# A two-block transformer kernel: the first two output chunks run together behind y, and the end of the memory attention runs inside the first latent head's gate product

## The chip, the cores and the metric

The kernel runs on one core of a Trainium2 chip. The metric is the device time of one execution in microseconds. Three executions of the kernel before took 2343.36, 2345.44 and 2347.05 us, a median of 2345.44.

## The reference

The input is 512 tokens of width 2048. Block one is a pre-norm layer of sliding-window attention with sinks (32 query heads of 64, 4 key heads), a SiLU gate and an output matrix. Block two has two layers, each of latent attention (8 heads of 128 + 64), a short convolution and an attention over 256 memory tokens (4 heads), which are concatenated, gated and multiplied by an output matrix. Cut to what matters here:

```python
# block one
y = (o.astype(z.dtype) * jax.nn.silu(z)) @ w_out
x = x + rmsnorm(y, g_post[i])
# block two, layer l
q = (rmsnorm_2(q_lat, q_norm_g[l]) @ w_uq[l]).reshape(b, s, MLA_HEADS, QK_HEAD_DIM)
kv = (rmsnorm_2(kv_lat, kv_norm_g[l]) @ w_ukv[l]).reshape(b, s, MLA_HEADS, QK_NOPE_DIM + V_HEAD_DIM)
a_out = mla_attention(q, k, v)
m_out = memory_attention(q_mem.reshape(b, s, MEM_HEADS, MEM_HEAD_DIM), mem_n, w_mk[l], w_mv[l])
y = jnp.concatenate([a_out, c_out, m_out], axis=-1) * jax.nn.silu(gate)
o = y @ w_o[l]
x = x + rmsnorm_2(o, post_norm_g[l])
```

## The kernel before, in words

Activations lie transposed: 16 tiles of 128 features by 512 tokens (`KT` = 16). Every product is written as three matmuls on halves of the operands: each operand is split into `hi` (rounded to fp32r) and `lo` (the remainder), and TensorE (PE) adds hi·hi, hi·lo and lo·hi (`passes`, L415). Weights come in chunks of 128 output features by 2048 input features, 1 MB each. SyncE loads a chunk into one of two slots (`raw`), ScalarE (ACT) writes `hi` (`split`, L758), VectorE (DVE) writes `lo` (`split`, L1082), and PE runs 48 matmuls over it (`features`). A chunk that uses a slot must wait until PE has finished the chunk before last. PE's result lies in one of two accumulators in PSUM (`acc`) until ACT or DVE has read it (`evacuated`).

The orders of all engines are written out by hand and are tied by counting semaphores. An engine takes its instructions strictly in its own order, so a wait holds all that stands behind it.

Three places matter for the change.

The start of an output product (three times: behind block one, behind layer 0 and behind layer 1 of block two). The gated outputs y stand in `g`, 16 tiles. ACT writes `h_hi` from them (`y_hi_tile`, L768), DVE writes `h_lo` (`y_lo_tile`, L1258), and PE multiplies. `h_hi` and `h_lo` hold the normed input h until then, and the last gate's product reads h up to its end, so ACT waits for the end of it. PE's first output chunk waits for each y tile in turn (`ready`); the second one runs its 32 matmuls on hi weights first and its 16 on lo weights last (`features_low_last`, L429 to L433). Before them stand the values of the last pair or head (`values_first`, L549; `values_head`, L721), which give the last y tile.

The first latent head of each layer. Its projection (`project`) makes the head's queries and keys from the latents, 18 matmuls, and, for two heads at once, the rotary queries and the values in banks of `sc`, 36 matmuls. These banks hold the scores of the last memory head until then. So PE first transposes the last memory head's probabilities (`turn_mem`, L650) as soon as DVE has scaled them (L1471), and waits until ACT has copied the result to `ptm` (L1000). Behind the projection come the memory values (`values_mem`, L657), the first gate product of the head, the scores (`scores_head`, L701 and L702) and the second gate product, with the transposes of the head's probabilities before its tile 12 (`turn_head`, L710).

DVE's order in that head: the lo split of the first gate's weights, the rotation of the queries (L1481 to L1486), the lo parts of keys, queries and rotary queries (L1500 to L1504), the lo split of the second gate's weights, the copy of the memory values (L1460), the first gate's evacuation (L1513), the lo split of the next head's weights, the gate (L1519), the maximum of the scores (L1521) and the scaling of the probabilities (L1527). ACT's exponentials (L1043) lie between these two.

Of the kernel before, what the change touches and what calls it, by code (L numbers as in the profile page):

```python
# [22 lines left out]
def build(nc, xT, memT, mem, pos, gains, sinks, consts, window, w1, w2, out):  # L23
# [89 lines left out]
    FIRST_SQUARES = SQUARES[:2]  # L113

# [12 lines left out]
    with ctx:  # L127
# [104 lines left out]
        y_hi_done, y_done = sem("y_hi_done"), sem("y_done")  # L232
# [172 lines left out]
        def _(pe):  # L405
# [168 lines left out]
            features(z_b, h_hi, h_lo, meanwhile=[(13, lambda: turn_first(B))])  # L574
            values_first(B)

            def out_product(l):

                features(chunk2(l, WO), h_hi, h_lo, ready=lambda j: pe.wait_ge(y_done, l * KT + (j + 1)))
                features_low_last(chunk2(l, WO + 1), h_hi, h_lo)  # L580
                with pe.Fori(1, KT // 2) as i:
                    for p in range(2):
                        features(chunk2(l, WO + p, i, 2), h_hi, h_lo)

            with pe.Fori(0, LAYERS) as l:
# [85 lines left out]
                def project(c, j, free_banks):  # L672

                    begin(c)
                    w_hi, w_lo = hi[c.slot], lo[c.slot]

                    def product(to, at, x, first, last, w_moves=False):
                        w = slice(at, at + (2 * P if w_moves else P))
                        return passes(to, w_hi[:, w], w_lo[:, w], m_hi[:, x], m_lo[:, x], first, last, w_moves)

                    for k in range(QRT):
                        product(acc[c.slot][:, :], k * QW[j], tile(KVRT + k), k == 0, k == QRT - 1)
                    for k in range(KVRT):
                        ins = product(ov[1][:, :], UK[j] + k * P, tile(k), k == 0, k == KVRT - 1)
                    if j == 0:
                        free_banks()
                        for k in range(QRT):
                            product(bank(0), k * QW[j] + P, tile(KVRT + k), k == 0, k == QRT - 1)
                        for b in range(TB):
                            for k in range(KVRT):  # L690
                                ins = product(bank(1 + b // 2, 2 * P, b % 2 * 2 * P), UV + k * 2 * P,
                                              slice(k * S + b * P, k * S + (b + 1) * P), k == 0, k == KVRT - 1, True)
                    ins.then_inc(chunk_done, 1)
# [30 lines left out]
                def end_of_memory():  # L724
                    turn_mem(MH - 1)
                    pe.wait_ge(ptm_done, l * MH + MH)

                def head(i, j, first=False):

                    no = l * MLA + (i * 2 + (j + 1))  # L730
                    project(chunk2(l, HEAD + 3 * j, i, 6), j, end_of_memory if first else lambda: turned_read(no - 1))
                    if first:
                        values_mem(MH - 1)
                    else:
                        values_head(no - 1, 1 - j)
                    features(chunk2(l, HEAD + 3 * j + 1, i, 6), h_hi, h_lo)
                    scores_head(no, i, j)
                    features(chunk2(l, HEAD + 3 * j + 2, i, 6), h_hi, h_lo, meanwhile=[(12, lambda: turn_head(no))])
# [4 lines left out]
                with pe.Fori(1, MLA // 2) as i:  # L743
                    head(i, 0)
                    head(i, 1)
                values_head(l * MLA + MLA, 1)
# [6 lines left out]
        def _(act):  # L753
# [109 lines left out]
            turned_first(B, B + 1)  # L863
            tanh_first(B, z_b)

            def y_hi_tiles(nxt, last_ready):

                with act.Fori(0, KT // 2) as t:
                    y_hi_tile(t)
# [5 lines left out]

            act.wait_ge(y1, PAIRS)
            act.wait_ge(chunk_done, N1)
            act.wait_ge(x_stored, 16)
# [34 lines left out]
            with act.Fori(0, LAYERS) as l:  # L913
# [103 lines left out]
                def head(i, j, first=False, last=False):  # L1017
# [27 lines left out]
                    ins.then_inc(exp2, 1)  # L1045
                    act.wait_ge(turned2, no)
# [32 lines left out]
        def _(dve):  # L1079
# [158 lines left out]
            def gate_first(i, zc):  # L1238
                dve.wait_ge(chunk_done, zc.n + 1)
                dve.tensor_tensor(zt[:, :], acc[zc.slot][:, :], r_x[:, :], ALU.mult).then_inc(evacuated[zc.slot], 1)  # L1240
                dve.wait_ge(tanh1, i + 1)
# [47 lines left out]
            split(chunk2(0, WO + 1))  # L1289

# [35 lines left out]
            with dve.Fori(0, LAYERS) as l:  # L1326
# [161 lines left out]
                def head(i, j, first=False, last=False):  # L1488
# [39 lines left out]
                    ins.then_inc(probs2, 1)  # L1528
                    dve.wait_ge(turned2, no)
# [4 lines left out]
                    dve.tensor_tensor(dg[:, :], acc[gb.slot][:, :], r_h, ALU.mult).then_inc(evacuated[gb.slot], 1)  # L1534
                    dve.wait_ge(tanh2, no * 2)
# [134 lines left out]
```

## Time and profile before

| | |
|---|---|
| median of three executions | 2345.44 us |
| the profiled execution's own time | 2344.45 us |
| its span | 2342.6 us |
| PE busy | 2277.9 us (97%) |
| DVE busy | 1186.3 us (51%) |
| ACT busy | 798.8 us (34%) |
| GpSimd busy | 184.2 us (8%) |
| moved by DMA | 238.98 MB, mean 102 GB/s |
| mean granted clock of PE | 0.993 |

The span is that of the core; the execution's own time is 1.9 us longer. PE's busy time counts matmuls, whose durations overlap in a stream. Starts and ends in the timelines are microseconds from the span's start; what stands in brackets behind a row is the idle time of that engine before it and the instruction that ended it. The output products of block one, layer 0 and layer 1 start near 503, 1316 and 2133 us; the first latent heads start near 1002 and 1821 us.

### The profile page before, as it was taken

Reading aid. Unit: us, or ns where it says so; the run is one execution under the profiler, and the core shown is the slowest. Engines: PE = TensorE matmul, PEld = TensorE weight load, DVE = VectorE, ACT = ScalarE, POOL = GpSimd, SP = SyncE. Lnnn points to the kernel's source line nnn. Section 1 sums busy time; section 2 is a strip of 40 time slices with the busy share of each in tenths; the row PEclk is TensorE's granted clock in tenths of the full one; section 3 lists DMA queues with packets and bytes.
Section 4 is the critical chain, followed back from the end, with each engine's and each line's share of the span. In section 5 each row is a group of like instructions: output and inputs, shape, how many; then the busy total and the mean of one; then the engine's idle time right before and its main releaser. Section 6 shows DMA issues by size and latency. Waiting matters only on the chain.

```text
span 2342.6 us, 28762 instructions
## 1 busy us (share of the span) xinstructions
PE 2277.9 (97%) x10726; PEld 1863.3 (80%) x10726; DVE 1186.3 (51%) x1531; ACT 798.8 (34%) x1216; POOL 184.2 (8%) x172
## 2 busy tenths in 40 slices
PE   7999999999999999999999999999999999999995
PEld 6888888878888888878877788878888787877884
DVE  7666666772238543445455532475433544554124
ACT  5443434352335411332333322344113323333220
POOL 4111111101110100000000011101000000000113
PEclk9999999999999999999999999999999999999997
DMA  7321222223237232212221222462322221213221
GB/s 282 113 72 72 72 83 78 76 98 114 90 142 263 81 108 90 70 61 78 75 87 57 113 91 106 150 246 72 108 90 72 75 79 59 87 66 138 107 90 72
DMA packets 36648, 238.98 MB, mean 102 GB/s; under 512 B 4192, under 2 KB 4448, under 8 KB 12896
## 3 DMA queue, kind: packets, MB, share of 16 engines
q1 hardware_dynamic: 29808, 204.47, 24.2%
q10 hardware_dynamic: 6336, 25.17, 2.8%
q0 software_dynamic: 432, 8.39, 0.9%
q8 instruction: 44, 0.72, 0.1%
q14 instruction: 28, 0.23, 0.0%
HBM read 221.24 MB, written 16.78 MB: 102 GB/s over the span
## 4 chain that ended last, share of the span: by engine, by line
PE 85%; DVE 7%; ACT 4%; issue 2%; DMA 1%; ACTq 0%; SPq 0%; POOL 0%; DVEq 0%; POOLq 0%
PE acc L415 68%; PE sc L415 4%; PE ov L721 2%; PE ov L415 2%; PE sc L710 1%; ACT hi L758 1%; ACT prob L1043 1%; PE ov L549 1%; PE sc L537 1%; DMA raw<-w_dram 1%; DVE lo L1082 1%; PE acc L429 1%; PE acc L430 1%; PE acc L433 1%; DVE st L1521 1%
## 5 line engine op out<-in xcount | busy, mean ns | idle before, releaser
L415 PE MATMUL acc<-h_hi,hi 128*128 128x512 f32 x2480 | 985.3, 397 | 27.3 <-DVE h_lo L1144 15.0
L415 PE MATMUL acc<-h_lo,hi 128*128 128x512 f32 x2480 | 967.8, 390 | 0.0
L415 PE MATMUL acc<-h_hi,lo 128*128 128x512 f32 x2480 | 967.5, 390 | 0.0
L1082 DVE TENSOR_TENSOR lo<-raw,hi 128x2048 fp32r<-128x2048 f32 (+2 forms) x196 | 432.7, 2208 | 492.1 <-ACT hi L758 489.8
L415 PEld LDWEIGHTS acc<-h_hi,hi 128*128 128x128 f32 x2480 | 467.1, 188 | 135.5 <-issue 28.8
L415 PEld LDWEIGHTS acc<-h_lo,hi 128*128 128x128 f32 x2480 | 467.2, 188 | 98.7 <-issue 5.3
L415 PEld LDWEIGHTS acc<-h_hi,lo 128*128 128x128 f32 x2480 | 466.8, 188 | 98.2
L758 ACT ACTIVATE hi<-raw 128x2048 fp32r<-128x2048 f32 (+2 forms) x196 | 361.5, 1844 | 275.2 <-PE acc L415 225.5
L765 ACT ACTIVATE sq<-acc 128x512 f32<-128x512 f32 x48 | 28.7, 599 | 358.5 <-PE acc L415 334.7
L827 ACT ACTIVATE prob<-prob,st 128x256 f32<-128x256 f32 x128 | 63.3, 496 | 136.6 <-DVE st L1204 136.6
L321 POOL TENSOR_TENSOR sqacc<-sqacc,sq 128x512 f32<-128x512 f32 x42 | 54.6, 1300 | 402.4 <-ACT sq L765 402.4
L1043 ACT ACTIVATE prob<-sc,st 128x512 f32<-128x512 f32 x64 | 43.2, 689 | 80.6 <-DVE st L1522 80.6
L1036 ACT ACTIVATE sq<-sq 128x512 f32<-128x512 f32 x16 | 10.1, 632 | 142.4 <-DVE sq L1513 142.4
L721 PE MATMUL ov<-prob,v 128*128 128x512 f32 x128 | 57.5, 592 | 0.0
L1513 DVE TENSOR_TENSOR sq<-acc,g 128x512 f32<-128x512 f32 x16 | 11.1, 692 | 84.0 <-PE acc L415 84.0
L325 POOL TENSOR_TENSOR sqacc<-sq 128x512 f32<-128x512 f32 x3 | 3.9, 1290 | 544.2 <-ACT sq L765 544.2
L415 PE MATMUL sc<-hi,m_hi 128*128 128x256 f32 (+1 forms) x128 | 43.2, 337 | 0.8 <-DVE lo L1082 0.8
L377 POOL COPY vcur<-vall 128x256 f32 x32 | 20.0, 650 | 297.4 <-PE ov L549 297.0
L390 POOL DMA_DIRECT2D area<-memT_dram x2 | 1.2, 612 | 535.5 <-ACT h_hi L768 535.5
L415 PE MATMUL sc<-lo,m_hi 128*128 128x256 f32 (+1 forms) x128 | 43.0, 336 | 0.0
L415 PE MATMUL sc<-hi,m_lo 128*128 128x256 f32 (+1 forms) x128 | 43.0, 336 | 0.0
L821 ACT ACTIVATE q<-dg 64x512 fp32r<-64x512 f32 x32 | 20.2, 630 | 66.4 <-DVE dg L1230 66.2
(217 smaller groups left out, 2489.3 us busy)
## 6 DMA issues: line engine op xcount, KB each, us to landing
raw<-w_dram SPq DMA_DIRECT2D x172, 1024.0 KB, 4.7
xr<-residual ACTq DMA_DIRECT2D x16, 512.0 KB, 5.7
residual<-g ACTq DMA_DIRECT2D x16, 512.0 KB, 4.2
raw<-w_dram SPq DMA_DIRECT2D x8, 896.0 KB, 4.4
raw<-w_dram SPq DMA_DIRECT2D x8, 768.0 KB, 5.4
g<-xT_dram SPq DMA_DIRECT2D x4, 1024.0 KB, 11.3
residual<-g POOLq DMA_DIRECT2D x1, 4096.0 KB, 13.8
area<-memT_dram POOLq DMA_DIRECT2D x2, 2048.0 KB, 9.2
```

What stands on the lines that cost most here:

```text
L321: pool.tensor_tensor(to[:, :], to[:, :], sq[:, tile(slot)], ALU.add).then_inc(added, 1)
L415: ins = pe.matmul(to, a, b, start=first and n == 0, stop=last and n == 2)
L429: pe.matmul(to, w_hi[:, tile(k, P)], x_hi[:, tile(k)], start=k == 0, stop=False)
L430: pe.matmul(to, w_hi[:, tile(k, P)], x_lo[:, tile(k)], start=False, stop=False)
L433: ins = pe.matmul(to, w_lo[:, tile(k, P)], x_hi[:, tile(k)], start=False, stop=k == KT - 1)
L537: ins = pe.transpose(bank(kb, P, par * 256 + nxt * P), prob1[:, src:src + P], ident)
L721: ins = pe.matmul(ov[0][:, :], v[:, (2 * k + j) * P:(2 * k + j + 1) * P], prob2[:, tile(k)], start=k == 0, stop=k == TB - 1)
L758: act.activation(hi[c.slot][:, 0:width], raw[c.slot][:, 0:width], ACT.Copy).then_inc(hi_done, 1)
L765: act.activation(sq[:, tile(slot)], src, ACT.Square).then_inc(squared, 1)
L827: act.activation(prob1[:, tile(n, 256)], prob1[:, tile(n, 256)], ACT.Exp, bias=nm[:, n:n + 1], accum_out=ls[:, n:n + 1])
L1043: ins = act.activation(prob2[:, tile(b)], bank(b), ACT.Exp, scale=MLA_SCALE, bias=nm[:, b:b + 1], accum_out=ls[:, b:b + 1])
L1082: dve.tensor_tensor(lo[c.slot][:, 0:width], raw[c.slot][:, 0:width], hi[c.slot][:, 0:width].bitcast(F32), ALU.subtract).then_inc(lo_done, 1)
```

## The change

Output starts. ACT writes the first five y tiles (`EARLY`) into `h_hi` as soon as the last gate's product has read the lower half of h, which PE reports through a new semaphore, `h_half_read`. DVE writes the `h_lo` of four of them before it copies the transposed probabilities, and of the fifth behind the gate's evacuation. PE runs the first two output chunks together (`features_behind_y`): chunk c takes tile k as soon as it is there, and chunk d takes its two hi matmuls of tile k - 8 behind it; its last hi tiles and all its lo matmuls come at the end. The values of the last pair or head stand before tile 4 of chunk c. The last pass of PE's loop over head pairs is written out.

First latent head. The first gate product begins behind the 18 matmuls of the projection. The transposes of the last memory head stand before its tile 2; before its tile 6 stand the wait for `ptm`, the memory values and the 36 matmuls for the pair of heads. ACT's and DVE's orders in this head are as before.

```diff
-            def features(c, x_hi, x_lo, ready=None, meanwhile=()):
+            def features(c, x_hi, x_lo, meanwhile=(), last_reader=False):
 
                 begin(c)
                 for k in range(KT):
                     for pause, other in meanwhile:
                         if k == pause:
                             other()
-                    if ready is not None:
-                        ready(k)
                     ins = k_tile(c, k, x_hi, x_lo, k == 0, k == KT - 1)
+                    if last_reader and k == KT // 2 - 1:
+                        ins.then_inc(h_half_read, 1)
                 ins.then_inc(chunk_done, 1)
...
-            features(z_b, h_hi, h_lo, meanwhile=[(13, lambda: turn_first(B))])
-            values_first(B)
+            features(z_b, h_hi, h_lo, meanwhile=[(13, lambda: turn_first(B))], last_reader=True)
+
+            def high(c, k, first):
+                pe.matmul(acc[c.slot][:, :], hi[c.slot][:, tile(k, P)], h_hi[:, tile(k)], start=first, stop=False)
+                pe.matmul(acc[c.slot][:, :], hi[c.slot][:, tile(k, P)], h_lo[:, tile(k)], start=False, stop=False)
+
+            def low(c, k, last):
+                return pe.matmul(acc[c.slot][:, :], lo[c.slot][:, tile(k, P)], h_hi[:, tile(k)], start=False, stop=last)
+
+            def features_behind_y(l, p, before, last_values):
+
+
+                c, d, lag = chunk2(l, p), chunk2(l, p + 1), KT // 2
+                begin(c)
+                for k in range(KT):
+                    if k == 4:
+                        last_values()
+                    pe.wait_ge(y_done, before + (k + 1))
+                    ins = k_tile(c, k, h_hi, h_lo, k == 0, k == KT - 1)
+                    if k == KT - 1:
+                        ins.then_inc(chunk_done, 1)
+                    if k == lag:
+                        pe.wait_ge(hi_done, d.n + 1)
+                        pe.wait_ge(evacuated[d.slot], d.accs)
+                    if k >= lag:
+                        high(d, k - lag, k == lag)
+                for k in range(KT - lag, KT):
+                    high(d, k, False)
+                pe.wait_ge(lo_done, d.n + 1)
+                for k in range(KT):
+                    ins = low(d, k, k == KT - 1)
+                ins.then_inc(chunk_done, 1)
...
-                def end_of_memory():
-                    turn_mem(MH - 1)
-                    pe.wait_ge(ptm_done, l * MH + MH)
-
-                def head(i, j, first=False):
+                def head(i, j, first=False, last=False):
 
                     no = l * MLA + (i * 2 + (j + 1))
-                    project(chunk2(l, HEAD + 3 * j, i, 6), j, end_of_memory if first else lambda: turned_read(no - 1))
-                    if first:
+                    hc = chunk2(l, HEAD + 3 * j, i, 6)
+
+                    def end_of_memory():
+                        pe.wait_ge(ptm_done, l * MH + MH)
                         values_mem(MH - 1)
-                    else:
+                        project_pair(hc).then_inc(chunk_done, 1)
+
+                    ins = project(hc, j)
+                    if j == 0 and not first:
+                        turned_read(no - 1)
+                        ins = project_pair(hc)
+                    if not first:
+                        ins.then_inc(chunk_done, 1)
                         values_head(no - 1, 1 - j)
-                    features(chunk2(l, HEAD + 3 * j + 1, i, 6), h_hi, h_lo)
+                    features(chunk2(l, HEAD + 3 * j + 1, i, 6), h_hi, h_lo,
+                             meanwhile=[(2, lambda: turn_mem(MH - 1)), (6, end_of_memory)] if first else [])
...
+                features_behind_y(l, N2 + WO, l * KT + KT, lambda: values_head(l * MLA + MLA, 1))
...
+            def early_y_hi_tiles(gates):
+
+
+                act.wait_ge(h_half_read, gates)
+                for t in range(EARLY):
+                    y_hi_tile(t)
...
+            act.wait_ge(x_stored, 16)
+            act.wait_ge(y1, EARLY + 1)
+            early_y_hi_tiles(1)
+            turned_first(B, B + 1)
+            tanh_first(B, z_b)
...
             y_first(A)
+            for t in range(EARLY - 1):
+                y_lo_tile(t, t + 1)
             turned_first(B)
-            gate_first(B, z_b)
-
-            def y_lo_tiles(before, last):
-
-                with dve.Fori(0, KT - 1) as t:
-                    y_lo_tile(t, before + t + 1)
+            gate_first(B, z_b, lambda: y_lo_tile(EARLY - 1, EARLY))
+
+            def y_lo_tiles(before, nxt, last):
+
+                for t in range(EARLY, KT - 4):
+                    y_lo_tile(t, before + (t + 1))
                 last()
-                y_lo_tile(KT - 1, before + KT)
-
-            y_lo_tiles(0, lambda: y_first(PAIRS - 1))
-            split(chunk2(0, WO + 1))
+                for t in range(KT - 4, KT):
+                    y_lo_tile(t, before + (t + 1))
+                split(nxt)
```

The same two moves stand in the last latent head: `early_y_hi_tiles(l + 2)` on ACT between the exponentials and the wait for the transposes, four `y_lo_tile` on DVE in front of its copies and the fifth behind the second gate's evacuation.

PE's order at the first latent head before. In the names, `acc1<-h_hi_55,hi1_52` is the first gate's product, `sc<-cst_61,prob_m_86` the transposes, `ov0<-ptm_102,mv_103` the memory values, and `sc<-` from `m_hi_58` the 36 matmuls for the pair; rows in a row of the same kind are left out.

```order
L415 MATMUL ov1<-m_hi_58,lo0_53 128x512
L650 MATMUL sc<-cst_61,prob_m_86 128x128 [waits probs_m]
L650 MATMUL sc<-cst_61,prob_m_86 128x128 x7
L415 MATMUL sc<-m_hi_58,hi0_51 128x512 [waits ptm_done]
L415 MATMUL sc<-lo0_53,m_hi_58 128x256
L657 MATMUL ov0<-ptm_102,mv_103 128x512 [waits om_done,ptm_done]
L415 MATMUL acc1<-h_hi_55,hi1_52 128x512 [waits evacuated1,lo_done]
L697 REGISTER_ALU [waits v_done]
L415 MATMUL sc<-kn_hi_106,qn_hi_105 128x512 [waits qk_done]
```

The same place in the change:

```order
L416 MATMUL ov1<-m_hi_58,lo0_53 128x512
L416 MATMUL acc1<-h_hi_55,hi1_52 128x512 [waits evacuated1,lo_done]
L681 MATMUL sc<-cst_61,prob_m_86 128x128 [waits probs_m]
L681 MATMUL sc<-cst_61,prob_m_86 128x128 x7
L416 MATMUL acc1<-h_hi_55,hi1_52 128x512
L688 MATMUL ov0<-ptm_102,mv_103 128x512 [waits om_done,ptm_done]
L416 MATMUL sc<-m_hi_58,hi0_51 128x512
L416 MATMUL sc<-lo0_53,m_hi_58 128x256
L416 MATMUL acc1<-h_lo_56,hi1_52 128x512
L729 REGISTER_ALU [waits v_done]
L416 MATMUL sc<-kn_hi_106,qn_hi_105 128x512 [waits qk_done]
```

The wait for the first gate's `lo` stands now directly behind the 18 matmuls of the projection, and the pair's 36 matmuls and the memory values stand inside the gate's product, 10 of its 16 tiles ahead of the scores.

DVE's order at the first output start before (`zt_65` and the second `sq_70` are the last gate, `g_57<-ov0` the last pair's y, `pt1_74` the transposed probabilities):

```order
L1220 SCALAR_TENSOR_TENSOR g_57<-ov1,sq_70 64x512
L1226 COPY pt1_74<-sc 128x512 [waits turned1]
L1240 TENSOR_TENSOR zt_65<-acc1,sqacc_69 128x512 [waits chunk_done]
L1242 SCALAR_TENSOR_TENSOR sq_70<-sq_70,zt_65 128x512 [waits tanh1]
L1258 ISA [waits y_hi_done]
L1258 TENSOR_TENSOR h_lo_56<-g_57,h_hi_55 128x512
L1220 SCALAR_TENSOR_TENSOR g_57<-ov0,sq_70 64x512 [waits sg_done,values1]
L1082 TENSOR_TENSOR lo1_54<-raw1_50,hi1_52 128x2048 [waits hi_done]
```

The same place in the change:

```order
L1271 SCALAR_TENSOR_TENSOR g_57<-ov1,sq_70 64x512
L1311 TENSOR_TENSOR h_lo_56<-g_57,h_hi_55 128x512 [waits y_hi_done] x4
L1277 COPY pt1_74<-sc 128x512 [waits turned1]
L1291 TENSOR_TENSOR zt_65<-acc1,sqacc_69 128x512 [waits chunk_done]
L1311 TENSOR_TENSOR h_lo_56<-g_57,h_hi_55 128x512 [waits y_hi_done]
L1295 SCALAR_TENSOR_TENSOR sq_70<-sq_70,zt_65 128x512 [waits tanh1]
L1311 TENSOR_TENSOR h_lo_56<-g_57,h_hi_55 128x512 [waits y_hi_done] x7
L1271 SCALAR_TENSOR_TENSOR g_57<-ov0,sq_70 64x512 [waits sg_done,values1]
L1133 TENSOR_TENSOR lo1_54<-raw1_50,hi1_52 128x2048 [waits hi_done]
```

Four tiles moved ahead of the copies of `pt1_74`, the fifth ahead of the gate's sum, and the last pair's y moved from behind tile 14 to behind tile 11.

## Rows read from the trace of the kernel before

**Rows 1.** The page, part 1: busy us, share of the span, instructions.
```profile
PE 2277.9 (97%) x10726; PEld 1863.3 (80%) x10726; DVE 1186.3 (51%) x1531; ACT 798.8 (34%) x1216; POOL 184.2 (8%) x172
```
**Rows 2.** Who waited for whom, PE: us in total, times, longest us.
```profile
PE acc L415 <- DVE h_lo L1258: 6.4, 8, 1.4
PE sc L415 <- ACT ptm L1000: 2.6, 2, 1.3
```
**Rows 3.** Chain of waits in order of time: start us, us.
```profile
530.33 152.32 PE acc L415 x672
```
**Rows 4.** Timeline of PE, first output start: start us, us, instruction [idle before].
```profile
503.48 1.74 PE L549 MATMUL ov<-pt,vcur 128*64 128x256 f32 x16 [0.59 <-issue]
...
530.16 0.39 PE L415 MATMUL acc<-h_hi,hi 128*128 128x512 f32 x1
```
**Rows 5.** Timeline of DVE and ACT, first output start.
```profile
502.09 1.29 DVE L1226 COPY pt<-sc 128x512 f32<-128x512 f32 x2
...
505.47 4.90 DVE L1258 TENSOR_TENSOR h_lo<-g,h_hi  x8
508.84 1.90 ACT L758 ACTIVATE hi<-raw 128x2048 fp32r<-128x2048 f32 x1
```
**Rows 6.** Timeline of PE, ACT and DVE, second output start.
```profile
1313.18 1.09 ACT L1048 ACTIVATE prob<-sc 128x512 f32<-128x512 f32 x2 [3.98 <-PE sc L710]
1313.18 1.29 DVE L1531 COPY prob<-sc 128x512 f32<-128x512 f32 x2 [2.06 <-PE sc L710]
...
1315.74 3.59 PE L721 MATMUL ov<-prob,v 128*128 128x512 f32 x8
...
1319.07 4.28 ACT L768 ACTIVATE h_hi<-g  x8 [1.78 <-DVE g L1539]
...
1343.88 0.39 PE L415 MATMUL acc<-h_hi,hi 128*128 128x512 f32 x1
```
**Rows 7.** Timeline of PE, first latent head of layer 0, then of layer 1.
```profile
1002.30 0.58 PE L415 MATMUL acc<-m_hi,hi 128*128 128x512 f32 x1
...
1007.88 1.09 PE L650 MATMUL sc<-cst,prob_m 128*128 128x128 f32 x8 [1.10 <-DVE prob_m L1471]
...
1042.91 1.91 PE L710 MATMUL sc<-cst,prob 128*128 128x128 f32 x16
...
1820.81 0.58 PE L415 MATMUL acc<-m_hi,hi 128*128 128x512 f32 x1
...
1828.78 0.50 PE L415 MATMUL sc<-m_hi,hi 128*128 128x512 f32 x1 [1.30 <-ACT ptm L1000]
...
1834.51 1.88 PE L657 MATMUL ov<-ptm,mv 128*128 128x512 f32 x4
...
1859.85 1.91 PE L710 MATMUL sc<-cst,prob 128*128 128x128 f32 x16
```
**Rows 8.** Timeline of DVE, first latent head of layer 1.
```profile
1826.78 2.29 DVE L1082 TENSOR_TENSOR lo<-raw,hi 128x2048 fp32r<-128x2048 f32 x1 [0.45 <-ACT hi L758]
...
1840.99 0.69 DVE L1504 TENSOR_TENSOR qr<-rot,qr 64x512 fp32r<-64x512 f32 x1
...
1845.26 0.68 DVE L1460 COPY g<-ov 128x512 f32<-128x512 f32 x1
1847.42 0.69 DVE L1513 TENSOR_TENSOR sq<-acc,g 128x512 f32<-128x512 f32 x1 [1.48 <-PE acc L415]
...
1851.88 2.29 DVE L1521 TENSOR_REDUCE st<-sc 128x4 f32<-128x2048 f32 x1 [0.78 <-PE sc L702]
...
1857.44 1.68 DVE L1527 TENSOR_SCALAR prob<-prob,st 128x512 f32<-128x512 f32 x4
```
**Rows 9.** A stop of PE at 1547; windows: busy us (instructions), granted clock.
```profile
1547.42 0.77 PE L415 MATMUL acc<-h_hi,hi 128*128 128x512 f32 x1 [3.32 <-DVE lo L1082]
...
1010.30:1014.30 4.00, 4.00 (x11) 0.57 0.28 98
1547.40:1552.80 5.40, 5.38 (x13) 0.50 0.70 224
```

More of the change, by code:

```diff
@@ L113, in build @@
     FIRST_SQUARES = SQUARES[:2]
+    EARLY = 5
     def sq_no(l, which):
@@ L670, in _, with product, project, project_pair @@
                     scores_mem(c)
-                def project(c, j, free_banks):
+                def product(c, to, at, x, first, last, w_moves=False):
+                    w = slice(at, at + (2 * P if w_moves else P))
+                    return passes(to, hi[c.slot][:, w], lo[c.slot][:, w], m_hi[:, x], m_lo[:, x], first, last, w_moves)
+                def project(c, j):
                     begin(c)
[L675 to L679, printed above, removed]
                     for k in range(QRT):
-                        product(acc[c.slot][:, :], k * QW[j], tile(KVRT + k), k == 0, k == QRT - 1)
+                        product(c, acc[c.slot][:, :], k * QW[j], tile(KVRT + k), k == 0, k == QRT - 1)
                     for k in range(KVRT):
[L684 to L693, printed above, removed]
+                        ins = product(c, ov[1][:, :], UK[j] + k * P, tile(k), k == 0, k == KVRT - 1)
+                    return ins
+                def project_pair(c):
+                    for k in range(QRT):
+                        product(c, bank(0), k * QW[0] + P, tile(KVRT + k), k == 0, k == QRT - 1)
+                    for b in range(TB):
+                        for k in range(KVRT):
+                            ins = product(c, bank(1 + b // 2, 2 * P, b % 2 * 2 * P), UV + k * 2 * P,
+                                          slice(k * S + b * P, k * S + (b + 1) * P), k == 0, k == KVRT - 1, True)
+                    return ins
                 def scores_head(no, i, j):
@@ L742, in _ @@
                 head(0, 1)
-                with pe.Fori(1, MLA // 2) as i:
+                with pe.Fori(1, MLA // 2 - 1) as i:
                     head(i, 0)
                     head(i, 1)
-                values_head(l * MLA + MLA, 1)
+                head(MLA // 2 - 1, 0)
+                head(MLA // 2 - 1, 1, last=True)
+                features_behind_y(l, N2 + WO, l * KT + KT, lambda: values_head(l * MLA + MLA, 1))
             out_product(LAYERS)
@@ L862, in _ @@
             tanh_first(A, z_a)
-            turned_first(B, B + 1)
-            tanh_first(B, z_b)
+            def early_y_hi_tiles(gates):
+                act.wait_ge(h_half_read, gates)
+                for t in range(EARLY):
+                    y_hi_tile(t)
             def y_hi_tiles(nxt, last_ready):
-                with act.Fori(0, KT // 2) as t:
+                for t in range(EARLY, KT // 2):
                     y_hi_tile(t)
@@ L1045, in head @@
                     ins.then_inc(exp2, 1)
+                    if last:
+                        early_y_hi_tiles(l + 2)
                     act.wait_ge(turned2, no)
@@ L1528, in head @@
                     ins.then_inc(probs2, 1)
+                    if last:
+                        for t in range(EARLY - 1):
+                            y_lo_tile(t, l * KT + (KT + t + 1))
                     dve.wait_ge(turned2, no)
```

18 lines of the change are left out of this document (10 added, 8 removed).

## The prediction

> **What bounds the kernel now.** I read the page's busy shares first: TensorE (PE) is busy for 2277.9 of the 2342.6 us of the span [rows 1], so only some 65 us are left to win and every stop of PE lengthens the run by about its own length. The view of who waited for whom says which stops the change aims at. The y tiles (h_lo at L1258) cost PE 6.4 us in 8 stops, and the transposed memory probabilities cost 2.6 us in 2 stops [rows 2]; before each of these last two there is a stop of 1.10 us for prob_m, as [rows 7] shows for layer 0. A long unbroken stretch of the chain of waits gives PE's pace: 672 matmuls of 512 columns in 152.32 us, 0.227 us each [rows 3]. A matmul's printed duration is longer (0.39 us), because the matmuls overlap. I therefore count from start to start, and I take a stage's cost as its own time less its matmuls at this pace. The timelines of PE, VectorE (DVE) and ScalarE (ACT) around the three starts of an output product and around the first latent head then give the rest.
>
> **Part 1: the first output start.** Before: the gate's last matmul leaves PE free at 502.7 (the start at 503.48, less its stop of 0.59 and the 0.17 by which a printed duration outlasts the pace), and the third output chunk begins at 530.16 [rows 4]. That is 27.4 us for 96 matmuls (21.8) and the values of the last pair (1.7). In the change the same matmuls remain, in another order. y tiles 0 to 3 are subtracted by DVE ahead of its copies of pt. DVE is free for them at 502.09, where the copies start now [rows 5]; eight y tiles take DVE 4.90 us [rows 5], 0.61 each, and ACT 4.28 [rows 6], 0.53 each. So the first is ready at about 502.8 and the four at 504.6; the pt copies (1.29) end at 505.8 in place of 503.4. PE loses 0.2 ahead of tile 0 and 0.2 ahead of the values. Tile 5 then needs the gate's evacuation, the tanh and the sum of it on DVE, 0.2. ACT must still split the weights of the second chunk between tiles 7 and 8 (1.90 us from 508.84, [rows 5]). In the change this split starts at about 508.7, no earlier than now, because tile 5 has to wait for the tanh; DVE ends tile 8 at 512.0, while PE with its 24 matmuls and the values is there at 510.6: a stop of 1.4. Behind that tile PE has five matmuls (1.13 us) for each tile against DVE's 0.61, so nothing else stops it. Sum: 23.5 of work, 2.0 of stops, 0.2 of restarts; 25.7 against 27.4. **Gain 1.7 us.** The bounds: none, if the y tiles also push back the tanh, and 3.7, if no stop is left.
>
> **Part 2: the two later output starts.** From the values of the last head to the third output chunk it takes 28.14 us now in layer 0 [rows 6], and layer 1 runs the same code. The work is 96 matmuls, 21.8, and the values at 3.4 (eight rows, 3.59 printed); the rest, 2.9 us, is stops and restarts. In the change five y_hi tiles (2.7 us) stand on ACT between the exponentials and the wait for the transposes, and four y_lo tiles (2.5 us) on DVE. ACT stands idle there for 3.98 us and DVE for 2.06 [rows 6], so DVE's copies come some 0.4 us later, still before the gate's product ends. PE now runs four tiles (2.7 us) and the values (3.4 us) before it needs tile 4, 6 us after the gate. ACT starts on the tiles that are left 3.3 us after the gate (1319.07 in rows 6, against 1315.74), as now; DVE ends tile 5 some 5 us after it and, with the weights' split between, tile 8 at 8.2, while PE wants this one at 8.9. No stop is left. **Gain 2 x 2.9 = 5.8 us**, with bounds of 2 x 1.5 (one stop of the first start's kind) and 2 x 2.9. That the loop's last pass is written out costs nothing that I can find: ACT and DVE have it written out already.
>
> **Part 3: the first latent head, where the change adds a wait.** Call the start of its projection 0. In layer 1 this is 1820.81, and the transposes of the head's own probabilities start 39.04 us later; in layer 0 it is 1002.30 and 40.61 [rows 7]. Now PE does 18 matmuls (4.3), stops for prob_m, transposes, stops for ptm and goes on with the pair of projections. In the change the gate product begins right behind the 18 matmuls, and it needs its own lo weights. DVE makes these only behind the prob_m scaling: from 1826.78 to 1829.07, 8.3 us after 0 [rows 8]; the change leaves the orders of ACT and DVE alone there. So PE stands from 4.3 to 8.5, **a stop of 4 us in place of two of 1.10 and 1.30**. The steps behind it: two tiles 1.5, eight transposes 0.8, four tiles 2.7, the values of memory 1.7 (1834.51 in rows 7, and the slower restart behind it), the pair 5.6 (1828.78 to 1834.51). The projection is complete at 20.9, not at 13.7. Two chains hang on this. The queries and keys are ready 7.2 us after it (1834.51 to the end of L1504, [rows 7, 8]); PE has only ten tiles left, 6.8 us, where it had 12.5 us of work: a stop of 0.5. Behind them DVE still has the lo split of the next gate and the memory copy, free at 11.4 (1845.94). It takes up the gate, which waited, and from there it needs 11.7 us to the end of the scaled probabilities, or 10.9 without its own 0.78 of waiting (L1513 to L1527, [rows 8]). So they come 22.4 after the projection; PE, with 20 and 36 matmuls, wants them at 20.0. **A second stop, 2.4 us.** The transposes start at 43.3: layer 1 loses 4.3 us, layer 0 loses 2.7, together **7.0 us**. The lower bound: if the split of the gate's weights came so early that PE never stood, both layers would gain their 2.4 and layer 0 another 1.6.
>
> **The clock.** In layer 0 the stops of 1.10 and 1.30 are followed by 4 us at a granted clock of 0.57, so mostly at 1.2 GHz in place of 2.4, and this is the 1.6 us by which layer 0 is slower than layer 1, where the same stops bring no drop. Behind the stop of 3.32 us at 1547 the clock stays at 0.50 for 5.4 us, 2.6 us lost [rows 9]. The change makes four longer pauses: twice 4 us, and twice 2.4 us with 16 transposes behind them. Nearest to the first two is the stop of 3.32, which brought the drop; nearest to the others is layer 0's pattern, which did so once in two. I take two drops at 2.1 us, the mean of 1.6 and 2.6: **4.2 us lost**. Bounds: none, and four of 2.6, 10.4. [...]
>
> **Sum:** -1.7 - 5.8 + 7.0 + 4.2 = +3.7 us, so 2348.2 on the profiled execution's own 2344.45. The three runs shown have their median 1.0 above that, at 2345.44; from there 2349.1.
>
> **The rivals.** (a) Slower: the clock also drops in the pauses at the turn of the first head's probabilities, three or four drops in all, +5.8 to +7.9, 2351 to 2353.5. It decides from the third drop on. For it: the low clock came after 2.4 us of stops with transposes between them in layer 0. Against it: it did not in layer 1. (b) The clock drops at most once: -0.5 to +1.6, 2345 to 2347. For it: layer 1. Against it: the stop at 1547. (c) Faster, the memory tail is covered as the code intends, because the lo weights are ready when the gate begins: -7.5 and -6.4 give 2331.5. The rows speak against it, since DVE's scaling and split stand in order; only an error of mine about that order allows it. (d) The change doesn't do what it says at the output starts: the early tiles come too late, and the gain there is 3, not 7.5: +8.2, 2353.6.
>
> **How the numbers follow.** Forecast (two drops) 0.38, (a) 0.33, (b) 0.19, (c) 0.05, (d) 0.05. No difference under 0.2% (4.7 us) can be told from none here; this limit lies at 2350.1, so (a), (d) and a small part of the forecast's case are slower, 0.44; (c) is faster, 0.05; the rest is 0.51. The range 2344.5 to 2354 takes in the forecast, (a), (b) and (d), and leaves (c) and the case of four drops at 2.6 outside.
>
> **What would show it.** In the changed kernel's list of PE's waits, the rows for ptm and prob_m are gone and two new stops of about 4 us for lo (L1133 there) stand at the first gate of each layer; two stops of about 2.4 for the probabilities follow 35 us later. The stops for y tiles shrink from 6.4 to about 2, all of it in the first start. From the values, or from the gate's end, to the third output chunk it takes 25.7 and twice 25.2. The windows behind the new stops show a granted clock near 0.5 to 0.6 in two places. If PE doesn't stand at the first gate, part 3 is wrong; if it does and no low clock follows, the clock term is.

## The result, and the profile after

The changed kernel took 2350.88 us in the median of 16 executions (2345.14 to 2354.23); the kernel before took 2345.32 in as many (2342.49 to 2348.36). The ratio is 1.0022, with a 95% interval of 1.0015 to 1.0030: slower by 5.6 us in the medians, and by 3.5 to 7.0 at the ends of the interval. The profiled execution took 2352.52 us, with a span of 2350.6, which is 8.0 more than the span before.

The page of the changed kernel, part 1 (busy us, share of the span, instructions) and part 3 (a DMA queue: packets, MB, share of 16 engines):

```profile
PE 2282.1 (97%) x10726; PEld 1866.7 (79%) x10726; DVE 1185.2 (50%) x1531; ACT 798.8 (34%) x1216; POOL 184.2 (8%) x172
...
q8 instruction: 50, 0.82, 0.1%
```

The count of matmuls is the one of [rows 1], and PE is busy 4.2 us longer with them; a matmul at half the clock is printed longer, so this is already a sign of more low clock. The other 3.8 us are longer stops. Where the releaser is given as "issue", the profile shows nothing that the engine waited for. The list of who waited for whom says which (us in total, times, longest us):

```profile
PE acc L416 <- DVE lo L1133: 13.8, 4, 3.8
PE sc L742 <- DVE prob L1583: 6.8, 10, 2.0
...
PE acc L416 <- issue: 2.0, 1, 2.0
...
PE acc L416 <- DVE h_lo L1311: 0.9, 1, 0.9
...
PE sc L416 <- DVE qr L1560: 0.5, 2, 0.2
```

The rows for ptm and prob_m are gone, and the y tiles cost 0.9 us in one stop where they cost 6.4 in eight [rows 2]. In their place stand two stops of 3.8 us for the gate's lo weights and two of 2.0 for the probabilities. One row has no counterpart in the prediction: a matmul of an output chunk that waits for "issue", 2.0 us.

Timeline of PE at the three output starts (start us, us, instruction, idle before): the first third chunk, then the turn of the last head's probabilities and the third chunk of layer 0, then of layer 1.

```profile
511.96 0.50 PE L416 MATMUL acc<-h_hi,hi 128*128 128x512 f32 x1 [0.95 <-DVE h_lo L1311]
...
528.44 0.39 PE L416 MATMUL acc<-h_hi,hi 128*128 128x512 f32 x1
...
1316.30 1.97 PE L742 MATMUL sc<-cst,prob 128*128 128x128 f32 x16 [0.71 <-DVE prob L1583]
...
1346.33 0.49 PE L416 MATMUL acc<-h_hi,hi 128*128 128x512 f32 x1
...
1350.43 0.50 PE L416 MATMUL acc<-h_hi,lo 128*128 128x512 f32 x1 [1.99 <-issue]
...
2168.54 0.39 PE L416 MATMUL acc<-h_hi,hi 128*128 128x512 f32 x1
```

And at the first latent heads of layer 0 and layer 1:

```profile
1002.17 0.58 PE L416 MATMUL acc<-m_hi,hi 128*128 128x512 f32 x1
...
1010.49 0.79 PE L416 MATMUL acc<-h_hi,hi 128*128 128x512 f32 x1 [3.84 <-DVE lo L1133]
1013.21 1.91 PE L681 MATMUL sc<-cst,prob_m 128*128 128x128 f32 x8
...
1032.97 0.50 PE L416 MATMUL sc<-kn_hi,qn_hi 128*128 128x512 f32 x1 [0.23 <-DVE qr L1560]
...
1047.98 1.97 PE L742 MATMUL sc<-cst,prob 128*128 128x128 f32 x16 [2.02 <-DVE prob L1583]
...
1832.83 0.80 PE L416 MATMUL acc<-h_hi,hi 128*128 128x512 f32 x1 [3.84 <-DVE lo L1133]
...
1870.44 1.97 PE L742 MATMUL sc<-cst,prob 128*128 128x128 f32 x16 [2.02 <-DVE prob L1583]
```

Windows of PE behind these stops (stretch, its length, busy us and instructions, granted clock, DMA share, GB/s):

```profile
1010.50:1014.00 3.50, 3.50 (x10) 0.50 0.39 112
1048.00:1053.00 5.00, 5.00 (x30) 1.00 0.02 3
...
1832.80:1837.00 4.20, 4.17 (x13) 0.50 0.30 94
1870.50:1875.00 4.50, 4.50 (x28) 1.00 0.02 4
...
1350.40:1355.00 4.60, 4.57 (x13) 0.63 0.37 112
```

Behind the stops of 3.84 the clock is granted at 0.50, so 1.2 GHz; behind those of 2.02 it stays full; behind the stop for "issue" it falls too.

Cut at the same instructions, the two profiled executions differ like this (us; the gate's end is worked out as in the prediction):

| stretch | before | after | difference |
|---|---|---|---|
| start to the end of block one's last gate | 502.73 | 502.85 | +0.1 |
| gate's end to third output chunk | 27.4 | 25.6 | -1.8 |
| third chunk to first latent projection, layer 0 | 472.1 | 473.7 | +1.6 |
| projection to turn of that head's probabilities | 40.6 | 45.8 | +5.2 |
| that turn to the turn of the last head | 268.3 | 268.3 | 0.0 |
| turn to third chunk, layer 0 | 32.7 | 30.0 | -2.7 |
| third chunk to projection, layer 1 | 476.9 | 478.2 | +1.3 |
| projection to turn | 39.0 | 45.9 | +6.9 |
| turn to turn of the last head | 268.2 | 268.3 | +0.1 |
| turn to third chunk, layer 1 | 32.7 | 29.8 | -2.9 |
| third chunk to the end | 181.8 | 182.1 | +0.3 |
| sum | 2342.6 | 2350.6 | +8.0 |

The changed starts give 7.4, and the changed head takes 12.1. What is left, 3.3, lies in stretches that the change doesn't name: +1.6 and +1.3 ahead of the projections, and small ones. These stretches vary by themselves: from the third chunk to the projection in layer 1, three profiles of the kernel before took 476.9, 476.5 and 474.0 us (experiment 6).

### The profile page after: what moved, and what is told of

Same layout as the page of the kernel before. It is cut to its first block, busy times and chain, and to the rows that moved or that the text cites. A ratio compares the mean times of both kernels' runs of the same rounds, so it can differ in the third digit from the quotient of the medians.

```text
span 2350.6 us, 28533 instructions
## 1 busy us (share of the span) xinstructions
PE 2282.1 (97%) x10726; PEld 1866.7 (79%) x10726; DVE 1185.2 (50%) x1531; ACT 798.8 (34%) x1216; POOL 184.2 (8%) x172
## 4 chain that ended last, share of the span: by engine, by line
PE 84%; DVE 8%; ACT 3%; issue 3%; DMA 2%; ACTq 0%; SPq 0%; POOL 0%; DVEq 0%; POOLq 0%
PE acc L416 67%; PE sc L416 3%; PE ov L753 2%; PE ov L416 2%; ACT hi L798 1%; PE sc L742 1%; ACT prob L1092 1%; DVE lo L1133 1%; DMA raw<-w_dram 1%; DVE st L1577 1%; PE ov L550 1%; PE sc L538 1%; DVE prob L1583 1%; PE sc L526 1%; DVE g L1184 1%
```

## The experiments

"Turn" is the start of the transposes of a head's probabilities, and where a time is given for "the head", it is that from the first latent head's projection to its turn, layer 0 first. Interval ratios are against the kernel before, measured beside each on the same chip.

**1. Each half alone.** `starts_only` has the new output starts and the old first latent head; in `memory_only` it is the other way round.

```diff
# starts_only, against the change
+                    if first:
+                        turn_mem(MH - 1)
+                        pe.wait_ge(ptm_done, l * MH + MH)
...
+                        values_mem(MH - 1)
-                             meanwhile=[(2, lambda: turn_mem(MH - 1)), (6, end_of_memory)] if first else [])
+                    features(chunk2(l, HEAD + 3 * j + 1, i, 6), h_hi, h_lo)
```

> The three output starts as in the change, the first latent head as before. Theory (the starts gain, the head loses): from the gate's end to the third output chunk it takes 25.6, 25.5 and 25.2 us as in the changed kernel (27.3, 28.1, 28.2 before), and the transposes of the first head's probabilities start 40.6 or 39.0 us after its projection, as before. The stop of 2 us without a releaser behind the second start (1350 us in the changed kernel), with the low clock behind it, belongs to the starts and stays: about 3.5 us faster than before, ratio 0.9985. Rival 1: that stop was a chance of one execution, and the sum is 7.4 us faster, ratio 0.997. Rival 2: the starts bring nothing, ratio 1.000.

> The first latent head as in the change, the output starts as before. Theory: PE stops 3.8 us for the lo weights of the first gate in each layer, and 2.0 us for the probabilities; the transposes start 43.3 us after the projection at full clock and 45.9 with the clock's drop behind the first stop. Slower than before by 5.2 to 6.9 us in each layer, 12 us in all, ratio 1.005. Rival (no clock term of its own): 7 us, ratio 1.003. The stop without a releaser near 1350 us isn't there.

Measured: `starts_only` 2335.69 us, ratio 0.9962 (0.9948 to 0.9975), so faster. `memory_only` 2356.74, ratio 1.0048 (1.0035 to 1.0062), slower. In `memory_only` the head takes 45.8 and 44.3 us from projection to turn, with the stops of 3.84 and 2.0, as in the changed kernel. In `starts_only` turn to third chunk takes 29.8 us in layer 0, where the changed kernel has 30.0, and the head 40.6 and 40.3, as before. So the two halves are separate, and the signs of both were as expected. The gain of the starts was larger than the 3.5 us expected (0.9985), and larger than its terms, 9.5 us by the medians where the three starts account for 7.4. And the row for "issue" came with the starts; `memory_only` doesn't have it:

```profile
1343.37 0.50 PE L416 MATMUL acc<-h_hi,lo 128*128 128x512 f32 x1 [2.33 <-issue]
...
1542.58 0.49 PE L416 MATMUL acc<-h_hi,hi 128*128 128x512 f32 x1 [1.65 <-DVE lo L1133]
```

The second of these rows of `starts_only` is where the surplus lies. It is the wait of the first product behind the next block's input, which in the kernel before took 3.32 us and brought 5.4 us of low clock [rows 9]; here it is 1.65, at full clock. From third chunk to projection in layer 1 `starts_only` took 474.3 us, against 476.9 before, although it pays 2.3 us for "issue" in it. No low clock followed that stop there (1343.3 to 1347.9 at 1.00).

**2. The stop for lo.** If PE stands at the first gate because DVE makes its lo weights behind the scaling of prob_m, an earlier split must take the stop away. `early_lo` lets ACT and DVE split these weights before the last memory head's exponentials, and no longer at their old place.

```diff
                     act.activation(qm[:, tile(c % 2)], acc[ch.slot][:, :], ACT.Copy).then_inc(evacuated[ch.slot], 1)
+                    if c == MH - 1:
+                        split(chunk2(l, HEAD + 1))
...
                     dve.tensor_tensor(nm[:, 0:TB], mx[:, 0:TB], r_minus, ALU.mult).then_inc(shift_m, 1)
+                    if c == MH - 1:
+                        split(chunk2(l, HEAD + 1))
```

> The changed kernel, but ACT and DVE split the first gate's weights before the last memory head's exponentials, where both wait. Theory (the stop is a matter of DVE's order): the stop of 3.8 us for lo is gone in both layers and with it the low clock; the projection is complete 16.7 us after its start, the stop of 2.0 us for the probabilities stays, and the transposes start at 39.1 in both layers instead of 45.8 and 45.9. 13 us less than the changed kernel, 7 to 8 less than before, ratio 0.997. Rival: the split delays DVE's maximum or ACT's exponentials for the memory head, the transposes of the memory head come late by up to 2 us, and the stop comes back there.

Measured: 2337.76 us, ratio 0.9969 (0.9959 to 0.9978), head 38.9 and 38.9. The stop of 3.84 is gone in both layers, the stop for the probabilities stays at 2.0, and the changed kernel's loss has become a gain. In layer 0 it brought the low clock, one of the two times that a stop of this kind did: the 16 transposes take 3.56 us in place of 1.97.

```profile
1039.42 3.56 PE L742 MATMUL sc<-cst,prob 128*128 128x128 f32 x16 [1.96 <-DVE prob L1589]
...
1853.60 1.97 PE L742 MATMUL sc<-cst,prob 128*128 128x128 f32 x16 [2.01 <-DVE prob L1589]
```

**3. What the low clock costs.** `filler` keeps the stop's length and takes away only its idleness: PE runs 16 more matmuls there, into the gate's accumulator, which the gate then starts afresh. The work is extra, and nothing of the computation is left out.

```diff
                     ins = project(hc, j)
+                    if first:
+                        ga = chunk2(l, HEAD + 1)
+                        pe.wait_ge(evacuated[ga.slot], ga.accs)
+                        for n in range(16):
+                            pe.matmul(acc[ga.slot][:, :], hi[hc.slot][:, 0:P], m_hi[:, tile(KVRT)], start=n == 0, stop=n == 15)
```

> The changed kernel with 16 matmuls of 512 columns put into the stop for the lo weights (they write the gate's accumulator, which the gate's own first matmul clears; nothing else is changed). Theory (half of the stop's cost is the clock): the filler takes 3.6 of the 4.2 us, the gate starts at the same time as in the changed kernel, the granted clock behind it is 1.0, and each layer's transposes start 43.3 us after the projection instead of 45.8 and 45.9: 5 us less than the changed kernel, about the time of before, ratio 1.000. Rival (the drop has nothing to do with PE's idleness, or the filler only adds work): the low clock stays, ratio 1.002 or more.

Measured: 2344.12 us, ratio 0.9996 (0.9986 to 1.0005), head 43.0 and 43.0. Timeline and window of `filler`, layer 0:

```profile
1007.46 3.79 PE L771 MATMUL acc<-m_hi,hi 128*128 128x512 f32 x16
1011.47 0.50 PE L416 MATMUL acc<-h_hi,hi 128*128 128x512 f32 x1 [0.22 <-DVE lo L1138]
...
1011.40:1016.00 4.60, 4.53 (x24) 1.00 0.28 85
```

PE does 3.6 us of useless work and waits 0.22 more, which is together the length of the stop, and the head is 2.8 and 2.9 us shorter than in the changed kernel's profile; the clock is granted in full behind it. So the stop itself costs what it lasts, and the low clock behind it comes on top. This alone brings the kernel back to a tie with the one before. By the medians it is 6.8 us, from 2350.88 to 2344.12, which is 1.1 more than the two heads show.

**4. The stop for "issue".** In the changed kernel, `starts_only` and `early_lo` it came at the ninth matmul of the third output chunk of the second start, never at the first or third. There PE's layer loop goes back to its top: in the change the loop ends with the first two output chunks and begins with the third. Theory: PE waits for its own instructions behind this long jump. The rival is a cause in the data (a weight chunk, a semaphore). `written_out` writes the two passes of PE's layer loop out, with the same matmuls on the same data.

```diff
-            with pe.Fori(0, LAYERS) as l:
+            for l in range(LAYERS):
```

> The changed kernel with PE's loop over the two layers written out, so that no branch goes back behind the second output start. Theory (the stop without a releaser is PE waiting for instructions behind the branch back): the stops of 2.0 us at the third chunk's third tile and the low clock behind it are gone, from the gate's end to the last matmul of the third chunk it takes 3 to 4 us less; ratio 1.001 against before, where the changed kernel has 1.002. Rival 1: straight code of twice the length brings such stops elsewhere, no gain. Rival 2: the stop has another cause (a weight or an accumulator) and stays where it is.

> The output starts alone, with PE's loop over the layers written out. Theory: 2 to 4 us less than the output starts alone (ratio 0.9962 there): 0.995. If the written-out code brings new stops: 0.996 or more.

Measured: `written_out` 2345.07 us, ratio 0.9997 (0.9988 to 1.0006); `starts_written`, which is `starts_only` with the same edit, 2332.24, ratio 0.9946 (0.9933 to 0.9960). No row for "issue" is left behind a start in either. Around the place in `written_out`:

```profile
1343.23 0.39 PE L416 MATMUL acc<-h_hi,hi 128*128 128x512 f32 x1
...
1345.04 0.39 PE L416 MATMUL acc<-h_hi,lo 128*128 128x512 f32 x1
...
1339.00:1347.00 8.00, 8.00 (x37) 1.00 0.41 141
```

The ninth matmul starts 1.81 us after the first, eight steps of 0.227, and the window has no gap. The edit also turns counts that the loop computes into constants, but these belong to the first pass as well, and there the third chunk has no stop (528.44 in the changed kernel). So the stop comes with the jump.

```profile
q8 instruction: 1, 0.02, 29.2%
...
q8 instruction: 1, 0.02, 1.2%
```

A packet of 16 KB starts in the first window, just before PE stands from 1348.44 to 1350.43. In all seven profiles with the stop such a packet starts 2.2 to 2.4 us before PE goes on with the ninth matmul. `written_out` has no packet of q8 from 1337 to 1354. The kernel before has its jump ahead of the first output chunk. Its row there, and its row of q8 in the window 1315 to 1320:

```profile
1320.64 0.50 PE L415 MATMUL acc<-h_hi,hi 128*128 128x512 f32 x1 [1.31 <-DVE h_lo L1258]
...
q8 instruction: 2, 0.03, 2.2%
```

By the medians the edit gives 5.8 us on the changed kernel, 5.6 on `early_lo_4` (experiment 5, both measured together) and 3.5 on `starts_only`, where the intervals of the two kernels overlap; 3 to 4, and 2 to 4 on `starts_only`, was expected, for the stop and the low clock behind it. In the profiles, third chunk to projection in layer 1 took 478.2, 475.6 and 476.1 us in three executions of the change (experiment 6) and 471.4 in `written_out`, so 4.2 to 6.8 lie in this stretch. Why it is more than the stop and its low clock is not shown.

**5. A version that beats both.** `early_lo_4` is `early_lo`, with the end of memory before the gate's tile 4 in place of 6, and DVE's copy of the memory values moved ahead of its wait for the projection, out of the chain to the probabilities. `early_lo_4_written` has PE's layer loop written out as well.

```diff
-                             meanwhile=[(2, lambda: turn_mem(MH - 1)), (6, end_of_memory)] if first else [])
+                             meanwhile=[(2, lambda: turn_mem(MH - 1)), (4, end_of_memory)] if first else [])
...
+                    if first:
+                        mem_out(MH - 1)
+                    else:
+                        split(ga)
```

> The changed kernel with the early split of the first gate's weights, the end of the memory attention before tile 4 of the gate's product instead of 6, and DVE's copy of the memory values before it waits for the projection. Theory (the second stop is the chain from the projection to the scaled probabilities, 22.4 us, against PE's work behind it): the projection is complete 15.6 us after its start, the probabilities 21.7 behind that, PE is there after 21.0; the stop shrinks from 2.0 to about 0.6, and the transposes start at 37.4 in both layers, against 39.1 with the early split alone and 39.0 and 40.6 before. Ratio 0.9955 to 0.996, 2 to 3 us below the output starts alone. Rival: PE now stops for ptm before tile 4, about 1 us, and nothing is won over the output starts alone.

> The same with PE's loop over the layers written out. If both theories hold their gains add: about 0.9945. If the written-out code brings new stops: as without it.

Measured: 2334.03 us, ratio 0.9950 (0.9936 to 0.9963), and **2328.48, ratio 0.9929 (0.9916 to 0.9943)**. The head takes 37.1 us in both layers of both kernels, and the stop for the probabilities is 0.6. What the two edits give singly was not tried. PE in `early_lo_4_written`, layer 0 and layer 1:

```profile
1037.21 1.97 PE L742 MATMUL sc<-cst,prob 128*128 128x128 f32 x16 [0.59 <-DVE prob L1589]
...
1846.42 1.97 PE L742 MATMUL sc<-cst,prob 128*128 128x128 f32 x16 [0.59 <-DVE prob L1589]
```

Beside it the kernel before took 2345.76, so this one is 17.3 us faster, and 22 faster than the change.

**6. The same kernels once more.** How constant is the low clock, and the stop for "issue"? Both kernels ran again, unchanged, for two more profiles each.

> The kernel before once more, for a second trace. What is in every execution: no stop without a releaser behind the output starts. What changes from one execution to the next by the theory: where the clock drops, and the length of the stops for lo at the first latent product (2.4 us in layer 0; 0.8 and 3.3 in layer 1). If the starts of the change shorten these (1.3 to 2.7 us in most of the kernels that have them), they are about as long here as in the first trace; if not, they lie anywhere between 1.3 and 4.

> A third trace of the kernel before. The same stops as in the second one are expected at the output starts; the stops for lo at the first latent product of each layer as long as there if they belong to the kernel, anywhere between 1.3 and 4 us if they belong to the execution.

> The changed kernel once more. In every execution: stops of 3.8 us for lo and 2.0 us for the probabilities in both layers, and the stop of about 2 us without a releaser at the third tile of the third output chunk of the second start. Likely in most: the low clock behind the stops of 3.8, 45.8 us from projection to transposes. If the stop without a releaser is missing, it is a matter of chance and not of the branch.

> A third trace of the changed kernel. The stop without a releaser is there again, 1.9 to 2.4 us at the same matmul, if it belongs to the branch; 45.8 us from projection to transposes where the clock drops, 43.1 where it doesn't.

Measured: before 2345.46 and 2346.28 us, after 2351.81 and 2350.12. The stop for "issue" came at the same matmul both times (2.32 us), and before has none there. The stops at the first latent head kept their length to 0.02 us; the clock behind them did not behave alike. The stop for lo behind layer 1's input, near 1547, took 3.32, 3.17 and 2.62 us in the three profiles of the kernel before, so its length is not fixed either.

The head:

| profiled execution | head, layer 0 | head, layer 1 |
|---|---|---|
| before | 40.6 | 39.0 |
| before_again | 40.5 | 39.0 |
| before_third | 40.5 | 40.6 |
| after | 45.8 | 45.9 |
| after_again | 44.7 | 45.4 |
| after_third | 45.8 | 45.4 |

The stops of 1.10 and 1.30 (before, and `starts_only`, `starts_written`) were followed by low clock 6 times in 10, for some 1.5 us each. The stops of 3.84 were followed by it all 10 times they occurred (the changed kernel three times, `memory_only`, `written_out`, two layers each), for 1.3 to 2.9 us over the 43.0 of `filler`, 2.3 in the mean. The stops of 2.0 brought it twice in 14: in `early_lo`, layer 0, and in `memory_only`, layer 1, where the 16 transposes take 2.81 us; both times the stretch from this turn to that of the last head took 270.0 us in place of 268.3.

## Why the prediction was right

The forecast, two drops of the clock and 2349.1 us, lies 1.8 under the measured median. That median is inside the range and 0.8 above the prediction's limit of 2350.1, so slower by just over 0.2%, the side that was held a little less likely than no difference. The sum was +3.7 against the profiled execution, which showed +8.0; by the medians it was +5.6.

- **Starts: right.** Gains of 1.8, 2.7 and 2.9 us stand against 1.7, 2.9 and 2.9. The one stop left is at tile 8 of the first start, 0.95 us for 1.4, where ACT's split of the second chunk's weights stands in the middle of the y tiles, as the prediction had it.
- **The stop at the first gate: right.** 3.84 us for 4, and `early_lo` shows its cause, the place of the lo split behind DVE's scaling.
- **The stop for the probabilities: right in place, 0.4 too large,** 2.02 for 2.4; that for the queries was 0.23 for 0.5. The head without its low clock takes 43.0 us (`filler`) where 43.3 was predicted.
- **The clock: two drops, as forecast.** In the profiled execution they cost 2.8 and 2.9 us, and over ten such stops 2.3, where the prediction took 2.1 each. It had to choose from two patterns and took their mean; the larger one, behind the stop of 3.32, was the nearer. The Trainium skill's page "TensorE: Matmul & The Clock Gate", section "Why this matters for your kernels", speaks against idle gaps between bursts of matmuls from a stated length on. The stops of 3.84 us are longer than that, and by that rule the clock falls behind them; the trace agrees, ten of ten. The shorter ones are not spared, as the rule would have it: low clock followed six of the ten pairs of 1.10 and 1.30 us, two of the fourteen stops of 2.0 and four of the seven for "issue". Rival (a), more drops at the turn of the probabilities, did not come in the change: none of its six such stops in three profiles brought one. But a third drop came, behind the stop for "issue" in all three, and 2350.88 us lies next to the 2351 of that rival.
- **The base of the head varies.** The prediction compared with 40.6 and 39.0 us. `before_third` shows 40.6 in layer 1 too: the low clock there comes and goes between executions of the same kernel, so one profile's 39.0 flatters the kernel before.
- **Missed: the jump.** The step that failed is the sentence that the written-out pass "costs nothing that I can find", and with it the count of stops behind the second start, none. The change moves the end of PE's layer loop from the values of the last head to behind two output chunks. There PE runs at full rate when the jump comes, and it stops for 1.99 us at the ninth matmul, with low clock behind it (4.6 us at 0.63 of the full speed, so some 1.7 us lost). `written_out` is 5.8 us faster than the change by the medians. In the kernel before, the jump lay directly ahead of the first output chunk, where PE stood 1.31 us for y in any case. Two packets of q8 start there between 1315 and 1320, before PE goes on at 1320.64; that the wait for instructions was covered by the values and by the wait for y is inferred from that, and was not tried by itself.
- **An unforeseen gain covers part of this.** In seven of the ten profiles with the new starts, two of the three of the change among them, the wait of layer 1's first product for its lo weights (near 1545) took 1.5 to 1.7 us; in the four profiles with the old starts (before three times, `memory_only`) it took 2.6 to 3.3. DVE's split waits there for ACT's, and ACT's for the DMA of the weights (4.88 us in the kernel before, 3.05 in `after_again`); what in the new starts moves it, some 200 us later, stays open. The profiled execution of the change is one of those without this gain (2.75 us), which is a part of why it shows +8.0 where the medians show +5.6.

So the sum was near, +3.7 for +5.6, with two errors in it of opposite sign: the jump, 3.5 to 5.8 us, and that gain. The gain can only be estimated. By the medians of `starts_only` it is 5.6 (9.5 measured, less the 7.4 of its terms, plus the 3.5 that its jump costs it). By the profiles it is 3.5: third chunk to projection in layer 1 took 475.7 us in the mean of the four with the old starts, and 472.2 in that of the three with the new starts and no jump. The terms that the prediction named came near what was measured; that the two it left out nearly cancel is luck.

## What to carry to other kernels

When work is moved under other work, ask what the covering work needs itself, and at which place of each engine's order that is made: here the gate product that was to hide a wait of 2.4 us began before its own weights were ready, and one split moved earlier turned a loss of 5.6 us into a gain of 7.4. Price a stop of TensorE as its length plus the low clock behind it, and expect that second part to vary between executions. And look where a long hardware loop jumps back: writing the passes out took the stop away here, and the loop of the kernel before, which jumps back where the engine waits anyway, showed none.

## What the runs showed of the hardware

PE's jump over a whole layer of its program stopped it for 2.0 to 2.3 us at the ninth matmul behind the jump, in six of the seven profiles that have the jump between two output chunks; in the seventh, `filler`, it was 0.82 at the first and 1.40 at the ninth. PE's short loops, the pairs of output chunks among them, jump back without a gap. The page of the profile shows more on the queue that brings instructions, 50 packets for 44, but `written_out` has 48 and no stop, so the number of packets isn't the price; the packet ahead of the stop starts only 2.2 to 2.4 us before PE goes on.

The Trainium skill's page "Runtime: NRT & Kernel Launch", section "Instruction fetch mechanics", says that a taken jump to a place outside the two pages at hand must fetch it by DMA before the engine goes on, and gives room for 2048 instructions on this engine. One pass of the layer's loop runs 3688 matmuls in the trace of the change (1346.33 to 2168.54); the loop over the output chunks alone repeats 96 of them six times, and by an estimate from this trace and the kernel's loops a third are repeats, so some 2400 are written in its program. By that rule a layer's instructions would not stay at hand, and a pair of output chunks, 96 matmuls, would; the trace agrees with both. The page gives no time for it; the 2.0 to 2.3 us are these runs' own.
